# The last tile's expert rows weighted by diagonal matrices on TensorE, all five final sums made in PSUM, and half of expert 30's own product ahead of its second tile

## What is computed

```
combine = einsum('tk,tke->te', wv, one_hot(eidx, N_EXPERTS))      # two weights per token
for e in range(N_EXPERTS):
    a = t @ w_gate[e];  u = t @ w_up[e]
    out = out + combine[:, e:e + 1] * ((silu(a) * u) @ w_down[e])
x = x + out
y = x * rsqrt(mean(x * x, axis=-1) + EPS) * final_norm_g
```

## Time and profile before

| | |
|---|---|
| device time, median of 3 runs | 777.6 us (777.34 to 778.83) |
| the profiled execution's own time | 776.52 us |
| its span in the profile | 774.8 us |
| TensorE (PE) busy | 668.8 us (86%) |
| VectorE (DVE) busy | 272.4 us (35%) |
| ScalarE (ACT) busy | 160.7 us (21%) |
| GpSimd (POOL) busy | 89.4 us (12%) |
| HBM read and written over the span | 235.65 MB and 19.20 MB, 329 GB/s |

### The profile page before, as it was taken

One profiled execution on the slowest core, in us unless ns is written; L12 is line 12 of the kernel. 1 busy time (PEld: TensorE's weight loads), 2 busy tenths in 40 slices (PEclk: granted clock), 3 DMA queues, 4 the chain that ended last, 5 costly groups with the idle time before them and its releaser, 6 DMA issues.

```text
span 774.8 us, 9756 instructions
## 1 busy us (share of the span) xinstructions
PE 668.8 (86%) x3294; PEld 333.8 (43%) x3294; DVE 272.4 (35%) x558; ACT 160.7 (21%) x314; POOL 89.4 (12%) x161
## 2 busy tenths in 40 slices
PE   6999989999996899999799987776778768888895
PEld 3488878954556533333233332222223322233231
DVE  7798994284476312121112121111111111112047
ACT  3677410421513001111001010010010101001023
POOL 4100000000000111212021211111121111021000
PEclk9999999999997799999999999999989999899998
DMA  9422016379217899999999999999999999999982
GB/s 332 183 109 110 1 53 278 117 290 383 91 61 287 309 353 377 412 389 415 382 419 397 408 412 408 415 406 411 413 393 415 401 412 408 402 403 415 422 331 110
DMA packets 29575, 246.56 MB, mean 318 GB/s; under 512 B 6578, under 2 KB 7090, under 8 KB 16592
## 3 DMA queue, kind: packets, MB, share of 16 engines
q1 hardware_dynamic: 22784, 233.95, 75.3%
q0 software_dynamic: 5280, 8.20, 3.1%
q10 hardware_dynamic: 1456, 3.62, 1.2%
HBM read 235.65 MB, written 19.20 MB: 329 GB/s over the span
## 4 chain that ended last, share of the span: by engine, by line
PE 46%; DMA 34%; DVE 9%; issue 3%; ACT 3%; PEldq 2%; ACTq 0%; PEld 0%; SPq 0%; POOLq 0%; DVEq 0%; POOL 0%
DMA mem<-in_w_down 33%; PE psA L1351 25%; PE psB L1351 20%; DVE mem L688 5%; PEldq L1684 2%; DMA mem<-hn_d,mem 1%; DVE mem L827 1%; PE psA L1356 1%; DVE mem L839 1%; ACT mem L629 1%; DVE mem L869 0%; DVE mem L870 0%; ACT front_c L618 0%; PEldq L1682 0%; ACT mem L566 0%
## 5 line engine op out<-in xcount | busy, mean ns | idle before, releaser
L1351 PE MATMUL psA<-mem 128*64 128x512 f32 (+8 forms) x1380 | 323.6, 528 | 43.6 <-DMA mem<-in_w_gu 12.4
L1351 PE MATMUL psB<-mem 128*64 128x512 f32 (+6 forms) x1242 | 274.4, 536 | 41.0 <-DMA mem<-in_w_gu 20.9
L1351 PEld LDWEIGHTS psA<-mem 128*64 128x64 f32 (+4 forms) x1380 | 154.2, 156 | 194.2 <-issue 163.8
L1351 PEld LDWEIGHTS psB<-mem 128*64 128x64 f32 (+2 forms) x1242 | 118.2, 153 | 178.9 <-issue 146.6
L688 DVE TENSOR_TENSOR mem<-mem 128x512 f32<-128x512 f32 (+18 forms) x121 | 66.0, 560 | 24.4 <-ACT mem L535 20.1
L1258 POOL DMA_INDIRECT y_d<-front_c,mem x30 | 27.5, 917 | 298.2 <-DVE front_c L1063 298.2
L1088 DVE TENSOR_TENSOR front_c<-front_c,psB 64x512 f32<-64x512 f32 x15 | 10.3, 690 | 136.1 <-ACT front_c L618 136.1
L1088 DVE TENSOR_TENSOR front_c<-front_c,psA 64x512 f32<-64x512 f32 x15 | 10.3, 690 | 124.6 <-ACT front_c L618 124.6
L1253 POOL DMA_INDIRECT mem<-hn_d,mem x34 | 33.4, 981 | 99.8 <-DMA hn_d<-mem 71.4
L618 ACT ACTIVATE front_c<-psA 64x512 f32<-64x512 f32 x15 | 8.8, 589 | 131.6 <-PE psA L1351 131.6
L618 ACT ACTIVATE front_c<-psB 64x512 f32<-64x512 f32 x15 | 8.8, 589 | 131.0 <-PE psB L1351 131.0
(11 more groups left out here) (232 smaller groups left out, 382.0 us busy)
## 6 DMA issues: line engine op xcount, KB each, us to landing
mem<-in_w_gu SPq DMA_DIRECT2D x64, 2048.0 KB, 36.6
mem<-in_w_down SPq DMA_DIRECT2D x32, 2048.0 KB, 41.8
mem<-in_w_out SPq DMA_DIRECT2D x2, 2048.0 KB, 8.4
y_d<-mem SPq DMA_DIRECT2D x1, 4096.0 KB, 11.8
mem<-y_d SPq DMA_DIRECT2D x8, 512.0 KB, 9.5
mem<-in_x_T SPq DMA_DIRECT2D x8, 260.0 KB, 8.7
mem<-in_w_vb SPq DMA_DIRECT2D x8, 256.0 KB, 8.9
mem<-in_x_prompt SPq DMA_DIRECT2D x4, 512.0 KB, 11.1
```

The source lines that it names most:

```text
L1351: return nc.tensor.matmul(out, lhsT, rhs, start=start, stop=stop, skip_group_check=True)
```

## The change

Four things change.

1. All five tiles are now summed in PSUM: `rest` (the identity times `x2`) runs for tiles 0, 1, 4 and 2, and `kept` is added on top. `add_kept` and `f_sum` are gone.
2. Tile 3, the last one, is no longer added up by DVE. DVE makes two 128x128 diagonal matrices of its weights (`cw_diag`), and TensorE computes per half: identity times `x2`, plus each diagonal times one of the two loaded rows, plus the kept rows (`weighted_rows`).
3. The order of the tiles at the end is 0, 1, 4, 2, 3 where it was 0, 1, 2, 4, 3.
4. At expert 30 the first half of its own `gate_up` runs ahead of the loop over its second tile and the other half behind it; the three `value_load`s stand ahead of expert 29's step; and in the second tiles of experts 30 and 31 TensorE runs 8 products of 128 columns without use (`keep_busy`) while it waits for the product of ACT and DVE.

```diff
@@ memory and tables
+        cw_diag = yin[:, 2 * NT, 0:256].rearrange("p (j c) -> p j c", j=2)
-        LAST_ORDER = (0, 1, 2, 4, 3)
+        LAST_ORDER = (0, 1, 4, 2, 3)
-        IN_PSUM = (0, 1)
@@ DVE
             dve.wait_ge(y_out[0], 16 * (NE // 2 - 1))
+            for j in range(2):
+                V.tensor_scalar(cw_diag[:, j, :], ident[:, :], cw[:, j, LAST_ORDER[-1]:LAST_ORDER[-1] + 1], None, ALU.mult)
             picks_of(0).then_inc(picks_rdy, 1)
...
-            for t in LAST_ORDER:
+            for t in LAST_ORDER[:-1]:
                 add_rows(t)
-            def add_kept(n, t):
-
-                dve.wait_ge(f_ps, n + 1)
-                dve.wait_ge(f_acc, n + 1)
-                x2t = x2[0:ROWS[t], t, :].rearrange("p (a n) -> p a n", a=2)
-                tt(x2t, x2t, LAST_PS[t], ALU.add).then_inc(f_sum, 1)
...
-            for n in range(2):
-                scaled(n, n)
-            add_kept(2, LAST_ORDER[2])
-            for n in range(3, NT):
-                add_kept(n, LAST_ORDER[n])
-                scaled(n - 1, LAST_ORDER[n - 1])
-            scaled(NT - 1, LAST_ORDER[NT - 1])
+            for n, t in enumerate(LAST_ORDER):
+                scaled(n, t)
@@ TensorE, second tiles and expert 30
+                    if turned or n_h:
+                        keep_busy(8, ps[:, 2, 0:128])
                     wait_before(xx_h, x + 1)
...
-            for s in range(2, NE - 2):
+            for s in range(2, NE - 3):
                 tile_step(s)
+            x0, x1, x2_ = (pe.value_load(xb[0:1, NE - 2 + k:NE - 1 + k], min_val=0, max_val=NX) for k in range(3))
+            tile_step(NE - 3)
             pe.wait_ge(h_done, NE - 2)
             h_T(psB[:, 2, :], hh[0:64, 1, :]).then_inc(hT_ps, 1)
             turn_rows(NE - 1)
-            x0, x1, x2_ = (pe.value_load(xb[0:1, NE - 2 + k:NE - 1 + k], min_val=0, max_val=NX) for k in range(3))
...
             down(psB[:, 3, :], hT[:, 1], NE - 3).then_inc(dn_ps, 1)
+            gate_up(psA[:, 1, :], xgT[:, 0], NE - 2, ks=range(4))
             further(x0, x1, psA, psB, NE - 2, NE, release=False, turned=True)
-            gate_up(psA[:, 1, :], xgT[:, 0], NE - 2).then_inc(gu_ps, 1)
+            gate_up(psA[:, 1, :], xgT[:, 0], NE - 2, ks=range(4, KD)).then_inc(gu_ps, 1)
@@ TensorE, the end
+            def weighted_rows(t):
+
+                pe.wait_ge(picks_rdy, 2)
+                pe.wait_ge(y_in[t], 48)
                 for h in range(2):
                     mm(LAST_PS[t][:, h, :], ident[:, :], x2[:, t, 512 * h:512 * h + 512], True, False)
+                    for j in range(2):
+                        mm(LAST_PS[t][:, h, :], cw_diag[:, j, :], yin[:, 2 * t + j, 512 * h:512 * h + 512], False, False)
+            rest(0, 0)
             pe.wait_ge(y_last, 2)
+            rest(1, 1)
+            pe.wait_ge(y_last, 4)
+            kept(0)
+            kept(1)
+            for n in range(2, NT - 1):
+                rest(n, LAST_ORDER[n])
+                kept(LAST_ORDER[n])
             pe.wait_ge(f_done, 1)
+            weighted_rows(LAST_ORDER[-1])
+            kept(LAST_ORDER[-1])
```

More of the change, by code:

```diff
@@ L261, in build @@
             sem, "x2_out zero_rdy zero_out tokens_rdy cw3_rdy cw_ps picks_rdy rest_out y_last".split())
[L262 removed]
+        f_acc, f_ps, f_sq, f_rt, f_done, f_out = map(sem, "f_acc f_ps f_sq f_rt f_done f_out".split())
         block = ctx.enter_context(nc.Block())
@@ L664, in _ @@
                 r = ROWS[t]
-                if t in IN_PSUM:
-                    act.wait_ge(f_ps, n + 1)
-                    total = LAST_PS[t]
-                else:
-                    act.wait_ge(f_sum, n + 1 - len(IN_PSUM))
-                    total = x2[0:r, t, :].rearrange("p (a n) -> p a n", a=2)
-                A(yin[0:r, 2 * t, :].rearrange("p (a n) -> p a n", a=2), total, ACT.Square, accum_out=fx[0:r, t:t + 1]).then_inc(f_sq, 1)
+                act.wait_ge(f_ps, n + 1)
+                A(yin[0:r, 2 * t, :].rearrange("p (a n) -> p a n", a=2), LAST_PS[t], ACT.Square, accum_out=fx[0:r, t:t + 1]).then_inc(f_sq, 1)
                 act.wait_ge(f_sq, n + 1)
@@ L1157, in add_rows @@
                 ins.then_inc(f_acc, 1)
[L1159 removed]
+            for t in LAST_ORDER[:-1]:
                 add_rows(t)
[L1162 to L1167 removed]
             def scaled(n, t):
                 r = ROWS[t]
[L1172 removed]
                 dve.wait_ge(f_rt, n + 1)
                 link(V.reciprocal(ss[0:r, 3, t:t + 1], ss[0:r, 2, t:t + 1]))
[L1175 removed]
+                V.scalar_tensor_tensor(x2[0:r, t, :].rearrange("p (a n) -> p a n", a=2), LAST_PS[t], ss[0:r, 3, t:t + 1],
                                        gfb[0:r].rearrange("p (a n) -> p a n", a=2), ALU.mult, ALU.mult).then_inc(f_done, 1)
             dve.wait_ge(rest_in, 16 * 5)
[L1179 to L1185 removed]
+            for n, t in enumerate(LAST_ORDER):
+                scaled(n, t)
         @block.gpsimd
@@ L1508, in logits, with keep_busy @@
                 ins.then_inc(lg_ps, 1)
-            def keep_busy(n):
+            def keep_busy(n, out=psB[:, 1, 0:128]):
                 for k in range(n):
-                    mm(psB[:, 1, 0:128], ident[:, :], ident[:, :], True, True)
+                    mm(out, ident[:, :], ident[:, :], True, True)
             def count_before(n, t):
@@ L1594, in x_T, with gate_up @@
                 return ins
-            def gate_up(out, xT, e, halfway=None):
-                for k in range(KD):
+            def gate_up(out, xT, e, halfway=None, ks=range(KD)):
+                for k in ks:
                     if k == 4 and halfway:
@@ L1728, in _, with rest, kept @@
             down(psB[:, 3, :], hT[:, 1], NE - 1).then_inc(dn_ps, 1)
-            def rest(t):
-                pe.wait_ge(f_acc, t + 1)
+            def rest(n, t):
+                r = ROWS[t]
+                pe.wait_ge(f_acc, n + 1)
+                for h in range(2):
+                    mm(LAST_PS[t][:, h, :], ident[0:r, 0:r], x2[0:r, t, 512 * h:512 * h + 512], True, False)
+            def kept(t):
+                for h in range(2):
+                    ins = mm(LAST_PS[t][:, h, :], picks[:, 128 * t:128 * t + ROWS[t]], yst[:, 1, 512 * h:512 * h + 512], False, True)
+                ins.then_inc(f_ps, 1)
+            def weighted_rows(t):
+                pe.wait_ge(picks_rdy, 2)
+                pe.wait_ge(y_in[t], 48)
                 for h in range(2):
                     mm(LAST_PS[t][:, h, :], ident[:, :], x2[:, t, 512 * h:512 * h + 512], True, False)
-            def kept(n, t):
-                for h in range(2):
-                    if n == 0:
-                        pe.wait_ge(y_last, 3 + h)
-                    ins = mm(LAST_PS[t][:, h, :], picks[:, 128 * t:128 * t + ROWS[t]], yst[:, 1, 512 * h:512 * h + 512], t not in IN_PSUM, True)
-                ins.then_inc(f_ps, 1)
-            rest(0)
-            pe.wait_ge(y_last, 2)
-            kept(0, 0)
-            rest(1)
-            kept(1, 1)
-            kept(2, LAST_ORDER[2])
-            kept(3, LAST_ORDER[3])
+                    for j in range(2):
+                        mm(LAST_PS[t][:, h, :], cw_diag[:, j, :], yin[:, 2 * t + j, 512 * h:512 * h + 512], False, False)
+            rest(0, 0)
+            pe.wait_ge(y_last, 2)
+            rest(1, 1)
[5 more added lines that the diff above has]
+                kept(LAST_ORDER[n])
             pe.wait_ge(f_done, 1)
-            kept(4, LAST_ORDER[4])
+            weighted_rows(LAST_ORDER[-1])
+            kept(LAST_ORDER[-1])
 _NAMES = ['x_prompt', 'x_sample', 'x_T', 'w_xa', 'w_ga', 'w_ub', 'w_vb', 'pack', 'b_T', 'c_T', 'ws_T', 'gmlp_norm_g',
```

3 lines of the change are left out of this document (removed).

## The result

The changed kernel takes 781.5 us (median of 18 runs, 777.58 to 783.33); the one before takes 777.12 us in as many runs beside it (775.01 to 781.43). The ratio is 1.0054, with a 95% interval of 1.0041 to 1.0066: slower by 3.2 to 5.1 us. Forecast were 781.4 us and +3.8 us.

A forecast was written before the change was run, and what follows sets the result against it. TensorE, full at the end, was taken to bound it: tile 1's `rest` at 753.5 us plus eleven groups of 18.9 us, then close and store, gave a span of 778.6, +3.8 us, so 781.4 us (range 779.4 to 783.7).

The forecast's parts named there:

- What bounds the end: At the end: DVE additions are in the last chain, but TensorE is full from 752.67 to 765.24 us.
- three signs that were to show the prediction wrong: Added MATMULs not 0.429 us apart, DVE's second tile not done at 753.4 us, or clock below full after 751 us.
- The price of a group: TensorE at the end: each group of four MATMULs, 0.429 us apart, costs 1.72 us.
- 18.9 + 0.16: TensorE at the end: eleven groups from tile 1's `rest` on take 18.9 us, the last row 0.16 us more.
- an 8x8 `rest`: Tile 4 at the end, a form no row shows: taken as 1.72 us, between 0 and 1.72.
- The pull-ahead: Around expert 30: expert 31's `down` ends 2.3 us earlier at full clock, 0.85 us earlier if the clock falls.
- the table loads cost nothing: Ahead of expert 29's step: their roughly 1.9 us fall into TensorE's 2.70 us wait for weights.
- it costs 0.2 us: `keep_busy` in expert 30's second tile: 1.7 us of products in a gap of 1.51 us.
- What the gain meets: At the end's first groups: TensorE waits some 1.2 us for DVE's sum of tile 1; 0.9 of 2.3 us survive.
- The later loads: Loads from `y2_d`, issued 1.3 us later, delay tile 1's sum by 0.3 us; possible range 0 to 1.3.
- The full queues: DMA share 1.03 from 741 to 751 us: later-issued loads stand behind older ones anyway, so delay taken nearer to nothing.
- The rule of the Trainium skill: Clock around 710 us: would fall as before, end still 781.4 us; the forecast took full clock as likelier, seven to three.

The follow-up runs named there:

- tail_only: Changed kernel with only the end changed, expert 30 left as in the kernel before; ratio to before 1.0059, or 4.6 us slower.
- dve_rows: Changed kernel without the diagonals, DVE adds tile 3's loaded rows too (ten groups on TensorE, not twelve); ratio to the kernel before 1.0017.
- mix: Changed kernel, but DVE adds kept rows of tiles 2 and 4 as before, only tile 3 by diagonals, order 0, 1, 2, 4, 3; ratio to before 0.9995.
- kept_first: Changed kernel with tile 0's `kept` moved ahead of tile 1's `rest`, as before the change; ratio to the kernel before 1.0045.
- small_last: Against mix_half: tile 4 of 8 rows comes last, and DVE adds tile 3's kept rows; ratio to the kernel before 0.9972.
- loads_late: Changed kernel with expert 30's three table loads back behind the turn of expert 31's rows; ratio to the kernel before 1.0056.
- mix_half: Against mix: DVE adds one of tile 3's two loaded rows, TensorE the other (nine groups on TensorE); ratio to the kernel before 0.9968.
- balanced_no_keep: Against mix_half: only `keep_busy` is removed; ratio to the kernel before 0.9991.
- no_keep_busy: Changed kernel without the eight `keep_busy` products in the second tile's loop; ratio to the kernel before 1.0055.
- balanced_old_front: Against mix_half: expert 30 as in the kernel before (no half ahead, table loads late, no `keep_busy`); ratio to before 0.9997.

## Why the prediction was right, point by point

**What bounds the end: right.** TensorE was full there and is so with the change, from DVE's sum of tile 1 on; tail_only alone gives +4.6 us. Of the three signs that were to show the prediction wrong none appeared: the added MATMULs start 0.43 us apart, the granted clock is 1.00 from 751 to 774 us, and DVE's second tile is done at 754.35 us, in a trace that ran 1.5 us late, against 753.4.

**The price of a group: right, a little low.** Forecast 1.72 us. Measured from start to start: 0.86 for each pair, and 1.79 to 1.82 for several whole groups (754.48 to 756.27, 759.80 to 761.61 to 763.42 to 765.24), though 1.72 for the one at 765.24. The extra 0.1 us stands mostly where the shape of the fixed matrix changes. From 754.48 to 773.99 it is 19.5 us where 18.9 + 0.16 was forecast, 0.5 us too little. The unseen form, an 8x8 `rest`, costs a full group, as taken.

**The pull-ahead: right in size and in all parts but one small one.** Forecast 2.3 us; 2.0 us measured (49.1 less 47.1) in dve_rows, mix, kept_first and small_last, 1.9 in the profiled run of the whole change. The early table loads and the full clock make it up, as in the forecast's sum, where the moved half had no term of its own: loads_late has it and gains nothing. So this part of the change, which gives the title its last words, did no work that any run shows. The forecast that the table loads cost nothing rests on a wait for weights; in two of the nine traces with early loads (the whole change and mix_half) they came after that wait had gone, and TensorE stood still 2.62 and 2.47 us, most of it for them. Of `keep_busy` I said that it costs 0.2 us. It costs 0.4 where the clock holds without it (47.1 against 46.7 in balanced_no_keep), and saves 1.3 where it doesn't (no_keep_busy).

**What the gain meets: right in kind, sized too high in the profiled run.** TensorE waits for DVE's sum of tile 1: 0.26 us there, 0.79 us in dve_rows, against 1.2 forecast. What of the 2.0 us arrives is small: tail_only and the whole change differ by 0.4 us, inside both intervals; 0.9 was forecast.

**The later loads: the term was too high.** I took 0.3 us. The loads were issued 1.9 us later (740.37 against 738.52) and even 2.8 us later in loads_late, and in the latter nothing arrived later; nor do the eleven traces show a landing that follows the issue. The full queues were the nearer row. That they are the reason is argued, not tried.

**The rule of the Trainium skill** (TensorE: Matmul & The Clock Gate, Part 4, PE-mode transpose), that turns do not count as a busy TensorE in the way products do, would have had the clock fall at 710 us in the changed kernel. It stayed full there in nine traces of nine with the loads early. Whether the turns held it or the `down` that moved up beside them is not told apart here.

The terms that were off are each below what the interval of the result can tell: a row of groups 0.5 us too short, and a surviving gain some 0.5 us too high even with the 0.3 us for the loads taken off it. Both make the forecast loss too small: +3.8 us, against 4.2 by the ratio. That 781.4 us lies 0.1 us from the measured 781.5 is luck, since the forecast started from 777.6 us for the kernel before, which then took 777.12. The span of 778.6 us was missed by 1.4, and the profiled run was already 1.5 us late at expert 27's `down`.

## What to carry to other kernels

Moving an addition from one engine to another's accumulator pays only as long as that engine has time left. Here five more groups of 1.72 us went to an engine that was done 3.5 us ahead of the last addition (765.24 against 768.76 us). The same idea with three fewer groups on TensorE (nine, not twelve) and three operations more on DVE (two `add_kept`, one loaded row of tile 3) turned +0.54% into -0.32%. So count both engines' sums to the last tile before moving work, and move single operations, not stages. A gain won ahead of such a join is worth little until the join no longer waits for the other side: the edit at expert 30 gave nothing that could be measured in front of DVE's sums, and by the medians about 2 us once the shares were even, with intervals that still overlap.

## What the hardware showed that I had not expected

- The same standstill of 1.5 us between two dense stretches was followed by the half clock in one trace (0.53 from 727 to 730 us in no_keep_busy) and by the full one in four (before, tail_only, balanced_old_front, balanced_no_keep). With products without use in the gap the clock was full in all eight traces. One in five against none in eight does not show that they held it.
- Ahead of expert 27's `down`, far from the changed places, the same splits by execution: after 1.48 us of standstill (the whole change), 1.74 (tail_only) and 2.05 (mix_half) it took 5.24 to 5.35 us, after 1.76 (dve_rows) and 1.92 (loads_late) 3.65. The length of the standstill alone does not tell what the clock does.
- Products of 8 rows by 8 columns took the same 0.43 us each as those of 128 by 128, but the clock fell (0.58 from 764.0 to 767.3 us) behind eight of them in small_last, though TensorE was busy all the time. In the whole change four such and four of 128 by 8 (759.80 to 763.42) were not followed by a fall. Each is one trace.
- A load issued 2.8 us later landed at the same time, with the queues full (DMA share 1.03 from 741 to 751 us).
- Three table loads hold TensorE's sequencer for 1.9 us. In nine traces with them early, seven hid them in a wait for weights and two did not.
